# First two mixer projections from unscaled x, small gates in 16 products, and the last pair of experts summed with tokens on partitions

## What is computed

```python
def rms_norm(x, w):
    y = xf * lax.rsqrt(jnp.mean(xf * xf, axis=-1, keepdims=True) + NORM_EPS)
    return (y * w.astype(jnp.float32)).astype(x.dtype)
...
for l in range(DEPTH):
    x = x + 0.5 * swiglu_ffn(rms_norm(x, ffn1_norm_w[l]), ...)
    x = x + hybrid_mixer(rms_norm(x, mix_norm_w[l]), l, w_in[l], ...)
    x = x + 0.5 * swiglu_ffn(rms_norm(x, ffn2_norm_w[l]), ...)
...
# hybrid_mixer: proj = h @ w_in, split in mlstm, ssm and attention parts and 16 small gate columns;
xbc = jax.nn.silu(causal_dwconv(xbc, conv_w, conv_b))
...
# expert_choice_ffn
ye = jnp.einsum('becf,efd->becd', hid, w_down) * top_aff[..., None]
combine = lambda ib, yb: jnp.zeros((L, D), yb.dtype).at[ib.reshape(-1)].add(yb.reshape(-1, D))
# and then: x = x + gate * combined, rms_norm(x, norm_f) is the output
```

## Time and profile before

| | us |
|---|---|
| median of 3 runs | 3370.78 |
| lowest and highest run | 3360.14, 3372.59 |
| the profiled execution | 3362.37 |
| its span, first to last instruction | 3360.3 |
| PE, DVE, ACT, POOL busy | 3113.0, 1640.4, 1038.7, 238.3 |
| mean granted clock of PE, in parts of 2.4 GHz | 0.954 |
| FFN 0 ends, Mixer 0's items begin (PE) | 428.7, 439.9 |
| FFN 2 ends, Mixer 1's items begin (PE) | 1656.0, 1665.3 |
| last product of the last wide ends | 3339.25 |

### The profile page before, as it was taken

One profiled execution on the slowest core, in us unless ns is written; L12 is line 12 of the kernel. 1 busy time (PEld: TensorE's weight loads), 2 busy tenths in 40 slices (PEclk: granted clock), 3 DMA queues, 4 the chain that ended last, 5 costly groups with the idle time before them and its releaser, 6 DMA issues. The chain is left out here.

```text
span 3360.3 us, 41902 instructions
## 1 busy us (share of the span) xinstructions
PE 3113.0 (93%) x17302; PEld 2367.6 (70%) x17302; DVE 1640.4 (49%) x3110; ACT 1038.7 (31%) x2121; POOL 238.3 (7%) x173
## 2 busy tenths in 40 slices
PE   8999999979999999999999879999898999888887
PEld 6777768857888878888788768888686888333333
DVE  5444474365555555545663555444654674211212
ACT  4222244343333243333344343222332553000002
POOL 0000032121000000000131220000000110000000
PEclk9999989879999999999998879999899998899999
DMA  4544421102223222222211112232212004899997
GB/s 184 189 158 156 148 79 40 51 26 85 97 82 116 85 94 82 76 70 82 76 63 51 38 38 77 93 112 83 80 62 76 2 2 176 360 421 421 421 421 306
DMA packets 66165, 443.36 MB, mean 132 GB/s; under 512 B 7477, under 2 KB 7733, under 8 KB 19641
## 3 DMA queue, kind: packets, MB, share of 16 engines
q1 hardware_dynamic: 61056, 423.65, 33.2%
q10 hardware_dynamic: 3224, 10.49, 0.8%
q0 software_dynamic: 1696, 6.55, 0.5%
HBM read 435.16 MB, written 5.51 MB: 131 GB/s over the span
## 5 line engine op out<-in xcount | busy, mean ns | idle before, releaser
L157 PE MATMUL ps<-b,b 128*128 128x512 f32 (+7 forms) x13990 | 2800.5, 392 | 160.4 <-DVE b L167 62.1
L157 PEld LDWEIGHTS ps<-b,b 128*128 128x128 f32 (+3 forms) x13990 | 2092.8, 183 | 833.6 <-issue 321.2
L167 DVE TENSOR_TENSOR b<-b,b 128x1024 fp32r<-128x1024 f32 (+9 forms) x736 | 602.2, 823 | 271.0 <-ACT b L387 161.3
L387 ACT CAST b<-b 128x1024 fp32r<-128x1024 f32 (+2 forms) x408 | 392.0, 962 | 444.0 <-PE ps L157 438.0
L167 DVE TENSOR_TENSOR b<-ps,b 128x64 f32<-128x64 f32 (+5 forms) x620 | 216.0, 364 | 310.9 <-PE ps L157 255.3
L167 POOL TENSOR_TENSOR b<-b,b 128x1024 fp32r<-128x1024 f32 (+3 forms) x120 | 204.0, 1715 | 1322.7 <-ACT b L387 892.2
L157 PE MATMUL ps<-b 64*64 64x64 f32 (+10 forms) x2848 | 260.6, 279 | 29.6 <-DVE b L177 15.6
L157 PEld LDWEIGHTS ps<-b 64*64 64x64 f32 (+3 forms) x2848 | 220.9, 162 | 66.2 <-issue 21.6
L177 DVE SCALAR_TENSOR_TENSOR b<-ps,b 128x512 f32<-128x512 f32 (+3 forms) x272 | 142.6, 547 | 212.1 <-PE ps L157 184.9
L183 ACT ACTIVATE b<-b 128x512 f32<-128x512 f32 (+8 forms) x294 | 156.2, 537 | 230.7 <-DVE b L177 188.5
L167 DVE TENSOR_TENSOR b<-b,ps 128x512 f32<-128x512 f32 (+1 forms) x106 | 71.8, 678 | 282.7 <-PE ps L157 272.9
(11 more groups left out here) (103 smaller groups left out, 551.9 us busy)
## 6 DMA issues: line engine op xcount, KB each, us to landing
b<-in_eg SPq DMA_DIRECT2D x64, 1024.0 KB, 27.4
b<-in_eu SPq DMA_DIRECT2D x64, 1024.0 KB, 27.2
b<-in_ed SPq DMA_DIRECT2D x64, 1024.0 KB, 27.0
b<-in_wg SPq DMA_DIRECT2D x44, 1024.0 KB, 4.8
b<-in_wu SPq DMA_DIRECT2D x44, 1024.0 KB, 4.9
b<-in_win SPq DMA_DIRECT2D x40, 1024.0 KB, 4.8
b<-in_wd SPq DMA_DIRECT2D x48, 768.0 KB, 4.2
b<-in_wmod SPq DMA_DIRECT2D x24, 1024.0 KB, 5.0
```

Source lines behind the costliest of these rows:

```text
L157: return e.h.matmul(out, l, r, start=start, stop=stop)
L167: return e.h.tensor_tensor(out, a, b, op)
L387: e.h.copy(hi, src).then_inc(*self.S.tick(("hi", i)))
```

## The change

1. `pre_next` is also true ahead of the two hybrid mixers. Items 0 and 1 take x times the norm's weight, unscaled (`raw`, `raw_pe`), and VectorE applies `rstd` when it reads their sums (`raw_read`). The scaled blocks for items 2 and on are made beside item 1 and item 2. The small gates come behind item 2 instead of item 0, their transposes and arithmetic behind item 3 instead of 1, the cumulative sums behind item 4 instead of 3, the biases behind 5 instead of 4. Convolutions 0 and 1 stand behind the scaling on VectorE.
2. The small gates' weights lie with hi and lo side by side (32 columns), so that the products with x's hi give both at once: 16 instead of 24. The transposes add the two sums, in 8 products of 16 columns for 512 tokens instead of 4 transposes.
3. In the last pair the roles of operands are exchanged (`z_pe`): tokens come out on partitions. During the pair x is transposed (`xt_pe`, 32 transposes), the modulation and norm rows are spread over the partitions (`row_pe`, 16 products), and copied by ScalarE. Behind the last half: `final_dve`, squares with sums on ScalarE, the root in two groups, the output by both engines, four transfers from SyncE. The stage Output is gone.

```diff
+    def pre_act(self, e, c):
...
+        e.wait_ge(self.before.x_there(c))
+        act(e, self.raw[c][0], self.k.xT[:, c, :], ACT.Copy, scale=self.k.col(f"nm_{self.l}", c)).then_inc(*self.S.tick(("rhi", c)))
+
+    def pre_dve(self, e, c):
+        e.wait_ge(self.S.at(("rhi", c)))
+        hi, lo = self.raw[c]
+        stt(e, lo, self.k.xT[:, c, :], self.k.col(f"nm_{self.l}", c), hi.bitcast(F32), ALU.mult, ALU.subtract).then_inc(
+            *self.V.tick(("raw", c)))
...
+    def raw_read(self, e, i):
+        e.wait_ge(self.P.at(("sum", i)), self.V.at("xzero"))
+        tt(e, self.put(i), self.k.bank[self.bank(i)][:, :], self.k.rstd, ALU.mult).then_inc(*self.V.tick(("put", i, 0)))
...
             if name == "norm":
-                self.norm_pe(e, B[7], 512, self.before.V.at(("add", 7)))
+                self.enter(e)
+                self.norm_sum(e, B[7], 512, self.before.V.at(("add", 7)))
+            elif name == "sum" and i == 0:
+                self.raw_pe(e, 0, range(8))
+            elif name == "sum" and i == 1:
+                self.raw_pe(e, 1, range(2))
+                self.norm_spread(e, B[7], 512)
+                self.raw_pe(e, 1, range(2, 8))
...
-                    if it.tag[0] == "xbc" and n:
-                        self.silu_act(e, n - 1)
+                    if it.tag[0] == "xbc":
+                        for c in {2: (0,), 3: (1, 2)}.get(n, (n - 1,)):
+                            self.silu_act(e, c)
...
+            elif name == "scale":
+                self.scale_dve(e, 512, k.xT, self.hp, lambda c: k.col(f"nm_{self.l}", c),
+                               behind={1: lambda: self.raw_read(e, 0), 5: lambda: self.raw_read(e, 1)})
+                for n in range(2):
+                    self.conv_dve(e, n, n)
...
-            a.pre_next = b.name[:3] == "ffn"
+            a.pre_next = b.name[:3] == "ffn" or b.name in ("mix0", "mix1")
```

The small gates, and the order on PE in the last pair:

```diff
         for k in range(8):
+            hi, lo = src(k)
             e.wait_ge(self.V.at(("h", k)))
-            p = mm3(e, bank[0:16, 0:n], (hi[:, k, :], lo[:, k, :]), src(k), k == 0, k == 7)
+            if k == 7:
+                mm(e, bank[0:16, 0:n], W[:, k, 0:16], lo, False, False)
+            p = mm(e, bank[0:32, 0:n], W[:, k, :], hi, k == 0, k == 7)
+            if k < 7:
+                mm(e, bank[0:16, 0:n], W[:, k, 0:16], lo, False, False)
...
+                if pr == 7 and m == 1:
+                    for j in range(4):
+                        self.row_pe(e, j)
+                if pr == 7 and m > 1:
+                    self.xt_pe(e, m - 2)
...
-        self.wide_pe(e, 7, 5, B[5], self.hidT[1], (0,))
-        self.y_pe(e, 7, range(4))
+        self.z_pe(e, 0)
         self.wide_pe(e, 7, 5, B[5], self.hidT[1], (1,))
-        self.y_pe(e, 7, range(4, 8))
+        self.z_pe(e, 1)
```

What VectorE does behind the down products (h is 0 or 1, half of the columns):

```diff
+            stt(e, t, B[4 + h][:, :], self.vT[:, 7:8], self.rows[h], ALU.mult, ALU.mult).then_inc(*V.tick(("t", h)))
+            e.wait_ge(S.at(("yhi", h)))
+            tt(e, self.ylo[:, cs], t, self.yhi[:, cs].bitcast(F32), ALU.subtract).then_inc(*V.tick(("ylo", h)))
+            for i in range(4):
+                x = self.xt[i][:, cs]
+                e.wait_ge(P.at(("z", h, i)), S.at(("xt", h, i)))
+                tt(e, x, x, self.zbank(h, i)[:, :], ALU.add).then_inc(*V.tick(("x", h, i)))
+                if h == 0:
+                    e.wait_ge(V.at(("x", 0, i)), S.at(("row", 2)), P.at(("w", 7, 3, 0)))
+                    tt(e, self.out[:, i, 0:512], x, self.rows[2], ALU.mult).then_inc(*V.tick(("n", i)))
+        self.final_mean(e, 0)
```

293 lines of the change are left out of this document (180 added, 113 removed).

## The result

The changed kernel took 3382.62 us in the median of 20 runs, the kernel before 3367.64 us beside it: **ratio of the means 1.0038, 95% interval 1.0025 to 1.0051, slower by 0.4%** (the medians' ratio is 1.0044), where 3365 us within 3347 to 3376 had been forecast. Two later measurements gave 1.0026 (1.0009 to 1.0044) and 1.0027 (1.0012 to 1.0042). The profiled execution took 3367.34 us (its span is 3365.3 us) where the sum had given 3356.3.

The account below looks back on a forecast made before the run. VectorE's chain was taken to bound the mixers' heads, weight waits and a chain of small steps the last pair. Gains of 1.6 (mixers), 2.3 (small gates elsewhere) and 2.2 (last pair) sum to 6.1 us: 3365 us, range 3347 to 3376.

Parts of the forecast that it names:

- What bounds the head: Mixer's head: VectorE's chain sets the end at 508, not TensorE at 461; TensorE's 15 us go into new waits.
- rival A: Mixers' heads: TensorE's idle time is really returned, 9.3 us per mixer, 27 us in all, 3344 us; chance 0.22.
- Later start of scaling: Seam from FFN to mixer: VectorE starts scaling 2.4 us later in mixer 0 and 3.4 in mixer 1.
- the term for the last two down products beside GpSimd's splits: End of the FFN before a mixer: each of these products costs VectorE 2.9 us against TensorE's 2.8.
- rival B: Seam before each mixer: GpSimd's two splits hold VectorE, each mixer loses 4.0 us, 3373 us; chance 0.15.
- a raw part of over 2 us: Seam before a mixer: VectorE's raw parts taking over 2 us beside GpSimd would show the forecast wrong.
- The chain from there: Mixer's head, scaling start to VectorE's last convolution: 67.4 us against 71.1, 3.7 won, with a 4.5 us gates wait.
- S: Moment VectorE starts scaling in a mixer's head; later steps are counted from it in us.
- Small gates elsewhere: Third mixer and context's part: 16 instead of 24 products save 2.3 us together, between 0 and 2.9.
- The last pair: End of the experts stage: TensorE ends 3.5 us later, the tail behind wins 5.7; net 2.2, between -1 and 5.7.
- the 6 us of cover: Last pair: TensorE's waits for weights, 1.31 us before each half, absorb 6 of 9.5 us of new work.
- Rival C: Last pair: no cover at all, last half ends 7 us late, tail -1.3 instead of 2.2, 3368 us; chance 0.08.

Follow-up runs that it names:

- heads_tail: Changed kernel with the small gates as in the kernel before (24 products, four transposes); ratio to the kernel before 0.9990.
- heads_only: Kernel before with only the change's first part, the new order at the two mixers' heads; ratio to the kernel before 1.0022.
- busy_wait: Changed kernel with 16 unread products of 512 columns on TensorE between item 3 and the gates' transposes; ratio to the kernel before 1.0009.
- mixed_b: Kernel before with the new last pair, and 16 products with four transposes for small gates in third mixer and context only; ratio to the kernel before 0.9985.
- tail_small_tr4: Kernel before with the new last pair, and small gates in 16 products with four transposes and one addition; old heads; ratio to the kernel before 0.9985.
- tail_only: Kernel before with only the change's third part, the new last pair without output stage; ratio to the kernel before 0.9986.
- copy_early: Changed kernel with VectorE's copy of the small gates moved between convolutions 0 and 1 in both mixers; ratio to the kernel before 0.9997.

## Why the prediction was wrong, point by point

- **What bounds the head: right.** VectorE's chain set its end, and TensorE's idle 15 us went into new waits. Of rival A (waits of TensorE truly returned) nothing came.
- **Later start of scaling: mis-sized, the step that failed first.** Forecast 2.4 and 3.4 us, measured 5.1 and 7.2 (against the same point of the FFN; 4.2 in mixer 0 in six other traces with the new heads, where one low stretch fewer lies ahead of it, 7.2 in mixer 1 in all with the low parts). The pace of 3.35 us between raw parts was right (415.08, 418.43, 421.78 in the trace after). What failed is the term for the last two down products beside GpSimd's splits, which I had added up to 2.9 us each from pieces of the seam between two FFNs, none of them beside a split. The last interval measured 5.94 (427.53 to 433.47; 5.84 in mixer 1), since the two splits stretched both the raw part and the addition. VectorE before shows such an addition already, with less to do there:

```profile
427.67 2.04 DVE L167 TENSOR_TENSOR b<-b,b 128x512 f32<-128x512 f32 x1 [0.70 <-ACT b L183]
```

  All seven intervals took 27.2 and 25.2 us, forecast 22.6; the kernel before took 22.1 and 19.1 for them, where I had reckoned with 19.6. From the last read to the start it is 8.0, not 7.3. That is most of rival B: the splits stretched the two operations by 3.2 us in mixer 0 and 3.1 in mixer 1, where it had 4.0; its sign, a raw part of over 2 us, was not met (1.76), since the larger share fell on the addition. By the rule of the Trainium skill (SBUF — State Buffer, section "SBUF: two separate sides") a VectorE operation with two SBUF inputs that comes behind a GpSimd one which reads SBUF waits until that instruction is done; the trace agrees: the splits end at 430.21 and 433.00, and the raw part and the addition, 0.75 and 0.69 us long alone, at 430.76 and 433.55.
- **The chain from there: the steps right, the clock left out.** Scaling ends at S+14.2 (forecast 14.6), the copy at S+28.7 (29.4), the wait at the gates is 4.21 (4.5), the gates are done at S+36.3 (36.8). Then item 4 is there at S+40.8 instead of S+35.6, as 10.2 us at half clock make it. I had priced what follows a wait of 4.5 us at full clock, with a row in front of me in which small jobs after waits ran at 0.50. The last convolution ended at S+69.8, and at S+68.9 in mixer 1. Where the clock did not fall so far the forecast of S+67.4 was met, partly by luck, since these kernels differ in the small gates or have 16 products more: heads_tail 67.25 (441.35 to 508.60), heads_only 67.3, busy_wait 67.0.
- **Small gates elsewhere: mis-sized.** In the third mixer eight products fewer brought TensorE to the transposes 1.6 us sooner (mixed_b, forecast 1.9), but nothing of it was left 10 us later; the eight products that replace the four transposes cost 1.3 to 1.5 us at half clock and not 0.3. In the context's part the stretch shrank by about 0.2 us with eight products and 0.9 with four transposes, forecast 1.0. And in the mixers, where I had seen them as part of a wait, they made it longer and the clock lower.
- **The last pair: right in kind, gain 5.3 us instead of 2.2.** Tail behind the last half: 15.5 us, forecast 15.3. But the last half is done only 0.2 us later than before, not 3.5. Timeline of TensorE after, last pair (answers the earlier trace rows):

```profile
3295.59 25.67 PE L157 MATMUL ps<-b,b 128*64 128x512 f32 x128 [1.31 <-DMA b<-in_eg]
3321.19 1.97 PE L286 MATMUL ps<-b,b 128*128 128x128 f32 x16
3323.09 7.09 PE L157 MATMUL ps<-b,b 128*64 128x512 f32 x32
3330.11 2.84 PE L286 MATMUL ps<-b,b 128*128 128x128 f32 x24
3333.67 16.16 PE L157 MATMUL ps<-b,b 128*64 128x512 f32 x72 [0.72 <-DVE b L3279]
```

  16 transposes in a row take 1.97 us, not four times 0.66, two halves 7.09, not 7.30: in these rows a group's duration holds more than its products' pace, once for each group, and I had multiplied it with every group. The second failed piece is the step from the last transposes to the down halves, 2.2 us by my sum for hidT and its copies behind ScalarE's eight; it is a wait of 0.72. So the down halves started at 3333.67 - 10.35 = 3323.3 in before's time and not at 3326.3, and run without a wait for weights: the 6 us of cover were nearly enough, and 5.7, the upper end that I had given, was nearly it. The last half ends at 3349.83, in before's time 3339.5, where it was 3339.25. Rival C is out.
- **The sum:** forecast were gains of 1.6, 2.3 and 2.2 us for mixers, small gates elsewhere and last pair. The first profile has a loss of 9.7 us for the mixers: 6.5 more than forecast by the start, 3.9 by the chain behind it, and 0.7 since mixer 1 before had 70.4 us from scaling to the last convolution and not mixer 0's 71.1, which I had taken for both. The small gates elsewhere are a loss of some 1.6 by the means of the traces (1.8 in the third mixer less 0.2 in the context's part), and the last pair is a gain of 5.3. The forecast's range reached 3376 since I let one rival at a time lose; it needed the start and the clock together.

**Open:** the mean granted clock of the kernels with 16 products for the small gates is 0.948 to 0.951 and of those with 24 it is 0.951 to 0.953; tail_small_tr4 and mixed_b, with old heads, are at 0.949. Within one kernel 0.001 goes with some 2.8 us, but between kernels it is no measure of time: these two have the ratio of tail_only, whose clock is 0.952. Nor do the ratios follow the heads closely (copy_early, above). The single traces, in which the untouched rests of the mixers differ by up to 12 us, don't say where the rest of the loss comes from. Why the low stretches there fall as they do was not tried.

## What to carry to other kernels

Work taken off an engine that waits for another at the next step need not be a gain: here it lengthened the wait from 2.52 to 4.21 us, and the granted clock behind it was 0.82 instead of 0.87 over 26 us, on the path. Follow the chain past the wait that an edit removes or makes, with the clock of the stretch behind it, and ask which later step of the other engine then decides. And where an engine has a collision already, an operation added beside it pays its own stretch too; take the price of short groups from rows in which they stand in a row.

## What was unexpected in the hardware

- 16 products without any use, put into a wait of 4.2 us, made the chain from scaling to the last convolution 2.9 us shorter in one mixer and 1.0 in the other (busy_wait against after): in the first the granted clock over the next 11 us was 0.99 instead of 0.56.
- Two executions of one program differ by 5.1 us over the 87 us behind mixer 0's head (clock 0.96 and 0.90), and executions of one kernel as a whole by about 2.8 us for each 0.001 of mean granted clock; that is the spread of 30 us.
- A VectorE operation with two inputs in SBUF and the addition behind it took 1.76 and 2.86 us beside two splits of 2.35 and 2.50 us on GpSimd, 3.2 us more than alone.
